# The second expert layer for the first 128 of 576 tokens: dense products against gathered table rows

## What is computed

```python
q = (xn @ w_q).reshape(bsz, t, P_HEADS, 2, P_QDIM // 2)          # 8 heads, 2 sides
s = jnp.einsum('bthcd,ckd->bthck', q, sub_keys)                  # 128 keys a side
sv, si = lax.top_k(s, P_TOPK)                                    # 16 a side, then 16 of 256 pairs
...
hid = jnp.einsum('td,ted->te', xb, u_tab[eb])                    # first expert layer
return jnp.einsum('te,ted->td', jax.nn.gelu(hid, approximate=False) * gb, v_tab[eb])   # second
```

## Time and profile before

| | busy us of 2449.8 | instructions |
|---|---|---|
| PE (matmul) | 2373.9 (97%) | 20030 |
| DVE | 1576.3 (64%) | 2909 |
| ACT | 955.2 (39%) | 1856 |
| POOL | 607.8 (25%) | 299 |
| DMA | 299.2 MB at a mean of 122 GB/s | 166063 packets |

### The profile page before, as it was taken

The page is one execution under the profiler, slowest core; times in us unless marked ns, Lnnn a source line. Parts: engine busy times, 40 slices in busy tenths (PEclk is TensorE's granted clock), DMA queues, the critical chain, the costliest instruction groups (busy, mean ns, idle before and its releaser), DMA issues.

```text
span 2449.8 us, 50410 instructions
## 1 busy us (share of the span) xinstructions
PE 2373.9 (97%) x20030; PEld 2323.9 (95%) x20030; DVE 1576.3 (64%) x2909; ACT 955.2 (39%) x1856; POOL 607.8 (25%) x299
## 2 busy tenths in 40 slices
PE   8997888989999999999999999999999999999998
PEld 7996777889999999999999999999999999999998
DVE  5545666576989859997544545444554445777776
ACT  5335554343333349998322222222222222222222
POOL 2434444224454541111311221112211120000000
PEclk9999999999999999999999999999999999999999
DMA  4441111332333326667523232332323323545551
GB/s 175 139 133 41 28 28 32 97 119 89 108 106 108 112 92 195 214 215 237 215 99 118 91 124 96 101 114 92 122 96 105 113 90 115 171 159 188 172 170 66
DMA packets 166063, 299.20 MB, mean 122 GB/s; under 512 B 12144, under 2 KB 103600, under 8 KB 161720
## 3 DMA queue, kind: packets, MB, share of 16 engines
q1 hardware_dynamic: 165944, 297.52, 36.3%
HBM read 233.18 MB, written 64.31 MB: 121 GB/s over the span
## 4 chain that ended last, share of the span: by engine, by line
PE 75%; DVE 2%; issue 1%; ACT 1%; POOL 1%; DVEq 0%; ACTq 0%; POOLq 0%
PE banks L123 23%; PE banks L125 23%; PE banks L124 23%; PE banks L2220 5%; PE banks L1923 1%; POOL u_low L2099 0%; DVE n_y L301 0%; DVE n_sq L342 0%; DVE gates_in L2609 0%; DVE res_lo L308 0%; DVE n_inv L294 0%; DVE gelu_out L2605 0%; DVE onehot_pairs L2308 0%; ACT res_hi L1780 0%; ACT wout_wh L1736 0%
## 5 line engine op out<-in xcount | busy, mean ns | idle before, releaser
L125 PE MATMUL banks<-w_high,v_low 128*128 128x288 f32 x2048 | 604.4, 295 | 0.0
L123 PE MATMUL banks<-w_high,v_high 128*128 128x288 f32 x2048 | 603.9, 295 | 0.4
L124 PE MATMUL banks<-w_low,v_high 128*128 128x288 f32 x2048 | 603.1, 294 | 0.0
L123 PE MATMUL banks<-res_hi,u_high 128*128 128x288 f32 x1456 | 441.6, 303 | 2.8 <-POOL u_low L2099 1.8
L124 PE MATMUL banks<-res_lo,u_high 128*128 128x288 f32 x1456 | 429.6, 295 | 0.0
L125 PE MATMUL banks<-res_hi,u_low 128*128 128x288 f32 x1456 | 429.5, 295 | 0.0
L123 PEld LDWEIGHTS banks<-w_high,v_high 128*128 128x128 f32 x2048 | 384.1, 188 | 3.7 <-DVE w_low L2522 3.7
L124 PEld LDWEIGHTS banks<-w_low,v_high 128*128 128x128 f32 x2048 | 384.1, 188 | 0.1
L125 PEld LDWEIGHTS banks<-w_high,v_low 128*128 128x128 f32 x2048 | 384.2, 188 | 0.0
L2546 DVE TENSOR_TENSOR res_x<-banks,res_x 128x288 f32<-128x288 f32 x496 | 217.9, 454 | 250.5 <-PE banks L125 250.5
L2099 POOL TENSOR_TENSOR u_low<-u_raw,u_high 128x1024 fp32r<-128x1024 f32 x71 | 181.2, 2552 | 686.3 <-ACT u_high L2095 686.3
(11 more groups left out here) (407 smaller groups left out, 4200.5 us busy)
## 6 DMA issues: line engine op xcount, KB each, us to landing
v_raw<-arg_v SPq DMA_DIRECT2D x128, 512.0 KB, 3.8
scratch_gates<-gate_stage SPq DMA_DIRECT2D x18, 2048.0 KB, 7.8
gates_in<-scratch_gates SPq DMA_DIRECT2D x32, 1152.0 KB, 7.1
u_raw<-arg_u SPq DMA_DIRECT2D x35, 1024.0 KB, 5.8
q_raw<-arg_u SPq DMA_DIRECT2D x38, 512.0 KB, 3.6
scratch_hidden<-gelu_ahead SPq DMA_DIRECT2D x56, 288.0 KB, 2.3
gelu_out<-scratch_hidden SPq DMA_DIRECT2D x56, 288.0 KB, 2.8
in_raw<-arg_w_in SPq DMA_DIRECT2D x25, 512.0 KB, 4.6
```

Of the source, the lines that this page charges most:

```text
L123: pe.matmul(out, ah, bh, start=first, stop=False)
L124: pe.matmul(out, ah, bl, start=False, stop=False)
L125: return pe.matmul(out, al, bh, start=False, stop=last)
```

## The change

- The first 128 tokens (`SP`) leave the dense second layer. Its products run over the other 448 (`DN`), in one piece: 128 keys x 8 channel blocks x 3 products of 128 x 448. All keys accumulate in the 8 banks, one bank for each channel block, so that nothing is added to `res_x` until the end.
- For that, the first layer of all keys is done before the second. The gated hidden values (`gated`) of all 128 keys are stored in DRAM (`scratch_prod`) and loaded again. The 52 keys of the first layer that were done early are loaded, gated and stored among the 76 others.
- The gates are spread for 448 tokens: `G_STEPS` is 7, `AHEAD5` 14, and 76 keys (19 groups) are left for `experts` where there were 72. The layout of the gates has tokens innermost in blocks of 32.
- For the 128 tokens, `place_picks` computes on DVE, with tokens on partitions, the row numbers of each token's 128 picks. After the last of the first layer's products POOL issues, for each pick number s of 128, four indirect DMAs (128 pieces of 1 KB each, one per token, from the table as it is laid out for the dense path) and one of 128 single hidden values (4 bytes): 640 indirect DMAs. DVE multiplies the values by the gates and adds row times weight to `row_total` (`accumulate`), 128 times 128 x 1024. These adds stand in DVE's order among the splits of key 9 to key 121 and wait for their rows; the ring holds 16 rows.
- The 128 hidden values of each key for these tokens are stored in a table of their own (`scratch_hid`), one more DMA for each key.
- The dense table `v` is still loaded whole, key by key, its 4 KB per partition now in four pieces of 1 KB.
- The last 3 keys run channel block by channel block; the 128 tokens are normalised on DVE, turned in 32 x 32 blocks and stored in 16 DMAs.
- No hardware loop is left in `experts`; all is written out.

The core of the diff:

```diff
-G_STEPS = TOK // (2 * TB)
+SP = P
+DN = TOK - SP
+NB = DN // TB
+G_STEPS = DN // (2 * TB)
...
+        self.hid = nc.dram_tensor("scratch_hid", (N_KEYS, P, SP), F32, kind="Internal").ap()
+        self.prod = nc.dram_tensor("scratch_prod", (N_KEYS, P, DN), F32, kind="Internal").ap()
+        self.gates = a["gates"].rearrange("g p t j -> g p (t j)")[:, :, 0:DN * JJ].rearrange(
+            "g p (n j t) -> g p n j t", j=JJ, t=TB)
...
+                    sp.dma_start(core.hid[KEY4 + n], gelu[:, n % 2, 0:SP]).then_inc(gelu_sent[n % 2], 16)
...
+            def place_picks():
...
+                link(dve.tensor_copy(sparse.expert[:, :], picks[:, 0, 1, :]))
...
+                dve.tensor_copy(sparse.expert[:, :], own).then_inc(sparse.ready, 1)
+                dve.tensor_copy(sparse.hidden[:, :], left[:, 2, :]).then_inc(sparse.ready, 1)
+                dve.tensor_copy(sparse.gate[:, :], picks[:, 0, 2, :]).then_inc(sparse.ready, 1)
...
-                    src = core.psum[:, g % BANKS, :].rearrange("p (t g j) -> p g t j", t=FOUR, j=JJ)
-                    act.activation(stage[:, b, :, r * FOUR:(r + 1) * FOUR, :], src, ACT.Copy).then_inc(staged, 1)
+                    src = core.psum[:, g % BANKS, :].rearrange("p (t g j) -> p g j t", t=FOUR, j=JJ)
+                    act.activation(stage[:, b, :, :, r * FOUR:(r + 1) * FOUR], src, ACT.Copy).then_inc(staged, 1)
...
+RING = 16
+CHUNK = 16
+V_SLOTS, W_SLOTS, G_SLOTS, H_SLOTS, M_SLOTS = 4, 3, 3, 3, 4
+NC_KEYS = KEY4
+TAIL = 3
+FIRST_OUT = NC_KEYS - W_SLOTS
+ACC_FROM, ACC_TO = 9, 122
...
+        def load_v(sp, k):
+            if k >= V_SLOTS:
+                sp.wait_ge(v_low, k - V_SLOTS + 1)
+            sp.dma_start(v_raw[:, k % V_SLOTS, :].rearrange("p (q d) -> p q d", q=4),
+                         a["v"][k // JJ][:, :, k % JJ * QW:(k % JJ + 1) * QW]).then_inc(v_in[k % V_SLOTS], 16)
+
+        def load_w(sp, k):
+            m = place[k]
+            sp.wait_ge(made_sent[m % M_SLOTS], 16 * (m // M_SLOTS + 1))
+            if k >= W_SLOTS:
+                sp.wait_ge(w_low, k - W_SLOTS + 1)
+            sp.dma_start(w_raw[:, k % W_SLOTS, :], core.prod[k]).then_inc(w_in[k % W_SLOTS], 16)
+
+        def send_made(sp, key):
+            m = place[key]
+            sp.wait_ge(made_done, m + 1)
+            sp.dma_start(core.prod[key], made[:, m % M_SLOTS, :]).then_inc(made_sent[m % M_SLOTS], 16)
...
+                if 1 <= n <= NC_KEYS:
+                    sp.wait_ge(gelu_done, n)
+                    sp.dma_start(core.hid[n - 1], gelu[:, (n - 1) % G_SLOTS, 0:SP]).then_inc(
+                        hid_sent[(n - 1) % G_SLOTS], 16)
+                    send_made(sp, n - 1)
...
+        def sp_out(sp):
+            for k in range(W_SLOTS, N_KEYS):
+                load_w(sp, k)
+                if k + 1 < N_KEYS:
+                    load_v(sp, k + 1)
...
+        def product(pe, k, dt):
+            w = slice(dt * P, (dt + 1) * P)
+            return three_products(pe, out_bank(dt), vh[:, k % V_SLOTS, w], vl[:, k % V_SLOTS, w], wh[:, k % W_SLOTS, :],
+                                  wl[:, k % W_SLOTS, :], k == 0, k == N_KEYS - 1)
...
+        def pe_out(pe):
+            for k in range(N_KEYS - TAIL):
+                pe.wait_ge(v_low, k + 1)
+                pe.wait_ge(w_low, k + 1)
...
+                    ins = product(pe, k, dt)
                 ins.then_inc(out_done, 1)
...
+        def split_w_high(act, k):
+            act.wait_ge(w_in[k % W_SLOTS], 16 * (k // W_SLOTS + 1))
+            if k >= W_SLOTS:
+                act.wait_ge(out_done, k - W_SLOTS + 1)
+            act.activation(wh[:, k % W_SLOTS, :], w_raw[:, k % W_SLOTS, :], ACT.Copy).then_inc(w_high, 1)
...
+        def accumulate(dve, s):
+            if s % CHUNK == 0:
+                weigh(dve, s // CHUNK)
+            dve.wait_ge(row_in[s % RING], 64 * (s // RING + 1))
+            if s:
+                dve.wait_ge(summed_rows, s)
+            else:
+                dve.wait_ge(rows_out, 1)
+            dve.scalar_tensor_tensor(out=total[:, :], in0=ring[:, s % RING, :], scalar=sparse.weight[:, s:s + 1],
+                                     in1=total[:, :] if s else rows[:, :], op0=ALU.mult, op1=ALU.add).then_inc(summed_rows, 1)
...
+        def dve_out(dve):
+            done = 0
+            for k in range(W_SLOTS, N_KEYS):
+                split_v_low(dve, k)
+                split_w_low(dve, k)
+                due = min(SEL, max(0, (k - ACC_FROM + 1) * SEL // (ACC_TO - ACC_FROM)))
+                for s in range(done, due):
+                    accumulate(dve, s)
+                done = max(done, due)
+            finish_rows(dve)
...
+        def pool_rows(pool):
+            def value(s):
+                pool.indirect_dma_start(
+                    out=sparse.value[:, s:s + 1], out_offset=None, in_=core.hid.rearrange("k p t -> (k p t)").unsqueeze(1),
+                    in_offset=bass.IndirectOffsetOnAxis(ap=sparse.hidden[:, s:s + 1], axis=0)).then_inc(
+                        values_in[s // CHUNK], 16)
+
+            def row(s):
+                if s >= RING:
+                    pool.wait_ge(summed_rows, s - RING + 1)
+                for q in range(4):
+                    pool.indirect_dma_start(
+                        out=ring[:, s % RING, q * QW:(q + 1) * QW], out_offset=None,
+                        in_=a["v"].rearrange("g p q (j d) -> (g p q j) d", d=QW),
+                        in_offset=bass.IndirectOffsetOnAxis(ap=sparse.expert[:, s:s + 1], axis=0),
+                        element_offset=q * JJ * QW).then_inc(row_in[s % RING], 16)
...
+            pool.wait_ge(hid_done, NC_KEYS)
+            for s in range(CHUNK):
+                value(s)
+            for s in range(SEL):
+                row(s)
+                if s + CHUNK < SEL:
+                    value(s + CHUNK)
```

More of the change, by code:

```diff
@@ L184, in __call__, with __init__ @@
         self.eng.wait_ge(self.sem, self.n)
+class Sparse:
+    def __init__(self, core, ctx):
+        self.expert = core.sb("expert_of_pick", [P, SEL], U32, ctx=ctx)
+        self.hidden = core.sb("hidden_of_pick", [P, SEL], U32, ctx=ctx)
+        self.gate = core.sb("gate_of_pick", [P, SEL], ctx=ctx)
+        self.value = core.sb("value_of_pick", [P, SEL], ctx=ctx)
+        self.weight = core.sb("weight_of_pick", [P, SEL], ctx=ctx)
+        self.ready = core.sem("picks_by_row")
 class Gemm:
@@ L2335, with __init__, made_at, experts @@
 Spread = namedtuple("Spread", "first_load first_low first_high first_gates sp pool pe act dve gates_stored gate_banks_read ahead_banks_read")
-def experts(core, acts, u, project, route, spread):
+RING = 16
[5 more added lines that the diff above has]
+ACC_FROM, ACC_TO = 9, 122
+class Products:
+    def __init__(self):
+        early = N_KEYS - NC_KEYS
+        self.loads = [[] for _ in range(NC_KEYS + 4)]
+        for e in range(early):
+            self.loads[e * (NC_KEYS - 3) // early].append(e)
+        self.order = []
+        for n in range(NC_KEYS):
+            self.order.append(n)
+            self.order += [NC_KEYS + e for e in self.made_at(n)]
+        self.place = {key: m for m, key in enumerate(self.order)}
+    def made_at(self, n):
+        return self.loads[n - 2] if n >= 2 else []
+def experts(core, acts, u, project, route, spread, sparse, ring, total, gelu_sent_ahead, mixing_sems):
     nc, a = core.nc, core.a
@@ new lines, in product @@
+        def product(pe, k, dt):
[6 more added lines that the diff above has]
+                pe.wait_ge(w_low, k + 1)
+                for dt in range(DT):
+                    if k == 0 and dt == 2:
+                        pe.wait_ge(rows_out, 1)
+                    if k == 0 and dt == 4:
+                        pe.wait_ge(gelu_done, NC_KEYS)
+                    ins = product(pe, k, dt)
+                ins.then_inc(out_done, 1)
+            for dt in range(DT):
+                for k in range(N_KEYS - TAIL, N_KEYS):
+                    if dt == 0:
+                        pe.wait_ge(v_low, k + 1)
+                        pe.wait_ge(w_low, k + 1)
+                    ins = product(pe, k, dt)
+                ins.then_inc(last_done, 1)
+            pe.wait_ge(last_added, 1)
+            pe.wait_ge(sq_added, DT - 2)
+            pe.matmul(out_bank(0), core.ones[:, :], squares[0], start=True, stop=False)
+            pe.wait_ge(squared, DT)
+            pe.matmul(out_bank(0), core.ones[:, :], square_of(DT - 1), start=False, stop=True).then_inc(sums, 1)
@@ L2730, in build @@
             mix(core, params, rows_of_tile, x, raw_ahead)
+            mixing_sems = range(first, core.sem("mixing_over").num + 1)
+        core.sems = ctx
+        with ExitStack() as place:
+            ring = core.sb("row_ring", [P, RING, D_MODEL], ctx=place)
+            total = core.sb("row_total", [P, D_MODEL], ctx=place)
         acts = Acts(core, ctx, "res", x)
         u = U(core, ctx)
+        sparse = Sparse(core, ctx)
         with ExitStack() as inner:
```

590 lines of the change are left out of this document (277 added, 313 removed).

## The result

The changed kernel takes 2678.3 us (median of 4 runs, 2666.3 to 2688.6) where the kernel before took 2453.6 in runs beside it: ratio 1.0907, 95% interval 1.0869 to 1.0945. It is 9% slower; the forecast was 3.5% faster.

The account below looks back on a forecast made before the run. PE bound the kernel before; after the change PE's own sum would be 2245 us, but POOL's indirect DMAs would bind the second layer: 1647 + 640 x 1.12 = 2364 us of span, 2368 us as median, range 2215 to 2720 us.

Parts of the forecast that it names:

- 205.5 ns a product: Second layer on PE: price of a 448-column product if all of it scales with width; 3072 products take 631.3 us.
- c: Time of one indirect DMA on POOL in the second layer, taken as 1.12 us, bounded by 0.36 and 2.55 us.
- PE's own sum: Whole kernel if PE alone binds: 2449.8 - 54.0 + 25.4 - 180.3 + 4.5 = 2245 us.
- The width of a product: Second layer on PE: 448 columns for 288 cost 132.1 to 205.5 ns a product, a change of -406 to -180 us.
- Nothing for `place_picks`, the row norm, the early keys, the stores: Small DVE work and extra SP loads and stores, all taken as hidden; `place_picks` some 5 us at worst.
- DVE's share and the transfers: Second layer: DVE needs 3.4 of PE's 4.9 us a key; DMA moves 163 MB at a share of 0.77 to 0.81.
- Rival 3: Second layer: transfers of small random pieces bind, share 1.09, stage 690 us, end at 2305 us; chance 0.08.
- the formula: End of the kernel when POOL's 640 indirect DMAs bind the second layer: 1647 + 640c us.
- Rival 2: Second layer: indirect DMAs and DVE obstruct each other, c 1.45 us, 2575 us; chance 0.40 together with a plain c above 1.27.
- The signs named in the forecast: Profile after: POOL issuing back to back from 1600 us, PE waiting for `w_low`; POOL gaps or c outside 0.93-1.25 us refute it.
- The range: Whole kernel: 2215 us (PE the bound) up to 2720 us (c = 1.67 us), a tenth left above, less below.
- The point from which c decides: Second layer: at c = 1.255 us the time equals the kernel before; rival 2 decides from 1.26 us on.

Follow-up runs that it names:

- without rows: Changed kernel without the 640 gathers and the 128 adds on DVE, so part of the work is missing: 2237.4 us, ratio 0.9104.
- the paced kernels: Changed kernel with another table layout, POOL's row gathers waiting for PE's keys: 4 KB rows (256 indirect DMAs) 2239.3 us; two 2 KB pieces (384) 2233.5 us.
- short pauses: Changed kernel with one memset of a spare tile on POOL (0.54 us) behind each row of five indirect DMAs: 2635.0 us.

## Why the prediction was wrong

The step that failed is the path from POOL's DMAs to PE. The forecast let them reach PE only through late rows, DVE's adds and `w_low`, and kept PE at 205.5 ns a product otherwise. In the changed kernel that path cost nothing; PE's own starts came late beside the indirect DMAs, 451 us in all. The price of a DMA, c, was mis-sized as well. Term by term:

- **PE's own sum: right.** Spreading steps of 27.0 us without a gap, seven of them; the first whole product at 1099.8 us (forecast 1103.6), the first product of 448 columns at 1596.0 (1598), span without rows 2235.7 (2245). The width of a product was the term with the widest bounds: 495 in 100 us are 202 ns, for 205.5 taken. By the Trainium skill (TensorE: Matmul & The Clock Gate, Back-to-back issue gap) the estimate was 199 ns; the run lies between the two.
- **Nothing for `place_picks`, the row norm, the early keys, the stores: right.** 1.6 us of waits in the second stage without rows.
- **DVE's share and the transfers: right.** An add took 1281 ns (1.38 taken, from the earlier trace rows), `w_low` 625 ns (0.58), and the DMA share was 0.81 to 0.86 in the paced kernels (0.77 to 0.81). Rival 3 falls by the 300 GB/s beside a busy PE.
- **c = 1.12 us: too small.** From the earlier trace rows, by the shortest wide operation of POOL's. Measured: 0.95 us busy and 0.30 us to the next start, 1.25 us, even with DVE idle. With that alone the formula gives 1647 + 800 = 2447 us, no change: this c by itself would not have made the kernel slower. The 0.30 us was seen nowhere in the trace of before: the earlier trace rows has 0.08 us between two operations. "About 1 us" (the Trainium skill, DMA: Bandwidth & Descriptors, Latency and other measured facts) meets the 0.95, not the distance; the page gives it for GpSimd's DMAs and doesn't set indirect ones apart, as the forecast had it.
- **Rival 2, DVE against POOL: right about POOL's queue and rated too low, but not what set this kernel's time.** It had c = 1.45 us and 2575 us. Where DVE works all the time the distance is 1.63 us; over a whole stage with POOL as the bound it is (2580.3 - 1598.4)/639 = 1.54 us with short pauses, some 1.43 without the 0.11 us that the memsets take. "A DMA issue doesn't read and write whole tiles" was the argument against, and it doesn't hold: the same 4-byte gather takes 0.94 us with DVE at rest and up to 2.1 us beside its work. Plain DMAs are not held up. The Trainium skill (SBUF — State Buffer, SBUF: two separate sides) says that a VectorE operation with two SBUF inputs locks the port that it shares with GpSimd only against a GpSimd operation that reads SBUF. That fits, since an indirect DMA takes its 128 indices from SBUF and a plain one doesn't; but many gathers took 0.94 us beside such operations too, and no run shows the port.
- **PE's slow stretches: missing, the step that failed.** The forecast knew PE only as waiting for semaphores, and put what the gathers do to PE's starts at nothing, without a word. In the changed kernel PE never waited for POOL's queue: when the last gather started, PE still had 111 us to run, and the end is 2235.7 + 451 us. A forecast with a c of 1.5 us, 2607 us, would have come near for another cause. POOL's queue alone would also have made the kernel slower than before: 2635 us with the short pauses, of which the memsets are some 70 us (an estimate, 0.11 us for each of 640 DMAs). The signs named in the forecast told it: POOL had gaps (93 us), PE didn't wait for `w_low`, and the clock fell without such a wait.
- **The range held by luck.** 2678 lies within 2215 to 2720, in the tail of rival 2, but the time came from a cause that no rival had. The point from which c decides, 1.255 us, wasn't tested, since POOL's queue was never the bound without the pauses.

## What to carry to other kernels

Count the indirect DMAs, not their bytes: each costs GpSimd 1.25 us, and 1.6 us in the mean beside a busy VectorE, whether it fetches 4 bytes or 4 KB for each of 128 partitions. So choose the table's layout so that one index fetches the whole row: here 256 for 640 turned 9% slower into 8% faster. And pace GpSimd by the engine that sets the time, so that it doesn't run ahead in bursts while VectorE is idle: that brought the last 30 us, to 9% faster.

## What the runs showed of the hardware

- TensorE can be slowed to a product in 0.7 to 2.8 us (0.203 us otherwise) with all semaphores met, while GpSimd issues indirect DMAs and VectorE is idle. The profile names it "issue". Weight loads and products are late alike, in steps of 0.70 us.
- Taking work off VectorE made a kernel slower by 73 us (one run each).
- Plain DMAs issued by GpSimd took 0.56 us each, beside a working VectorE too, and 512 of them did TensorE no harm. Indirect ones took 0.94 us with VectorE at rest and up to 2.6 us beside its work.
